# Second expert matrix loaded in 4 KB runs a partition apart, first products on neighbouring columns

## What is computed

```python
gate = jnp.sum(jax.nn.one_hot(eidx, N_EXPERTS, dtype=jnp.float32) * w[..., None], axis=1)
hg = jnp.einsum('td,edf->tef', h, p['w1'])
hu = jnp.einsum('td,edf->tef', h, p['w3'])
act = jax.nn.silu(hg) * hu * gate[:, :, None].astype(h.dtype)
routed = jnp.einsum('tef,efd->td', act, p['w2'])
```

## Time and profile before

| | |
|---|---|
| Median of three executions | 1235.48 us |
| The profiled execution, its own time | 1235.82 us |
| Its span, first to last instruction | 1234.1 us |
| Mean granted clock of TensorE | 0.983 of full |
| TensorE busy | 95% of the span |
| Bytes read from and written to memory | 322.21 MB, 33.30 MB |

### The profile page before, as it was taken

One profiled execution on the slowest core, in us unless ns is written; L12 is line 12 of the kernel. 1 busy time (PEld: TensorE's weight loads), 2 busy tenths in 40 slices (PEclk: granted clock), 3 DMA queues, 4 the chain that ended last, 5 costly groups with the idle time before them and its releaser, 6 DMA issues.

```text
span 1234.1 us, 26531 instructions
## 1 busy us (share of the span) xinstructions
PE 1167.9 (95%) x9397; PEld 847.9 (69%) x9398; DVE 563.0 (46%) x956; ACT 325.8 (26%) x633; POOL 514.3 (42%) x522
## 2 busy tenths in 40 slices
PE   4899999999999899999899999997989999899997
PEld 3599999999999899897755555544545554455542
DVE  4285676658568868337643322221112222222234
ACT  3522322323323451435121121111111111111122
POOL 2144444445448343600355444542344455344420
PEclk9899999999999899999999999998999999999999
DMA  9954345435421233548399999999999999999887
GB/s 307 324 177 147 86 146 166 140 91 160 151 81 41 69 85 101 143 168 338 127 405 410 401 397 412 411 414 415 413 411 413 411 413 399 411 415 410 342 319 267
DMA packets 149035, 337.48 MB, mean 273 GB/s; under 512 B 14807, under 2 KB 99363, under 8 KB 123369
## 3 DMA queue, kind: packets, MB, share of 16 engines
q1 hardware_dynamic: 129304, 296.57, 64.0%
q0 software_dynamic: 16656, 34.14, 7.3%
q10 hardware_dynamic: 3025, 6.07, 1.4%
HBM read 322.21 MB, written 33.30 MB: 288 GB/s over the span
## 4 chain that ended last, share of the span: by engine, by line
PE 74%; DMA 13%; issue 5%; DVE 4%; POOL 2%; SPq 1%; ACT 0%; DVEq 0%; POOLq 0%; ACTq 0%
PE ps L1882 23%; DMA w<-in_w_dram 10%; PE ps L1896 10%; PE ps L1602 9%; PE ps L1603 9%; PE ps L1604 9%; DMA ring<-in_w_ada_dram 2%; PE ps L1890 2%; PE ps L1746 1%; PE ps L1955 1%; PE ps L1615 1%; PE ps L1747 1%; PE ps L1750 1%; PE ps L1988 1%; PE ps L1544 1%
## 5 line engine op out<-in xcount | busy, mean ns | idle before, releaser
L1882 PE MATMUL ps<-w,xe 128*64 (+1 forms) x3136 | 378.2, 393 | 21.1 <-DMA w<-in_w_dram 19.2
L1882 PEld LDWEIGHTS ps<-w,xe 128*64 128x64 f32 x3136 | 221.6, 136 | 171.7 <-issue 55.8
L569 POOL TENSOR_TENSOR wsplit<-ring,wsplit 128x1024 fp32r<-128x1024 f32 x72 | 175.3, 2435 | 252.2 <-ACT wsplit L721 222.1
L1602 PE MATMUL ps<-h_s_hi,wsplit 128*128 128x260 f32 x960 | 272.3, 284 | 0.0
L1604 PE MATMUL ps<-h_s_hi,wsplit 128*128 128x260 f32 x960 | 270.8, 282 | 0.0
L1603 PE MATMUL ps<-h_lo_m_hi,wsplit 128*128 128x260 f32 x832 | 234.9, 282 | 0.0
L1464 DVE TENSOR_TENSOR rs<-sg,ps 128x128 f32<-128x128 f32 x98 | 28.2, 288 | 365.5 <-ACT sg L1051 365.5
L1602 PEld LDWEIGHTS ps<-h_s_hi,wsplit 128*128 128x128 f32 x960 | 180.8, 188 | 6.7 <-issue 5.9
L1896 PE MATMUL ps<-w,eactT 128*64 128x512 f32 (+1 forms) x784 | 184.8, 592 | 0.0
L1604 PEld LDWEIGHTS ps<-h_s_hi,wsplit 128*128 128x128 f32 x960 | 180.9, 188 | 0.0
L1603 PEld LDWEIGHTS ps<-h_lo_m_hi,wsplit 128*128 128x128 f32 x832 | 156.7, 188 | 0.0
(11 more groups left out here) (357 smaller groups left out, 1373.0 us busy)
## 6 DMA issues: line engine op xcount, KB each, us to landing
w<-in_w_dram SPq DMA_DIRECT2D x192, 1024.0 KB, 21.6
ring<-in_w_in_dram SPq DMA_DIRECT2D x56, 512.0 KB, 3.8
ring<-in_w_ada_dram SPq DMA_DIRECT2D x8, 2048.0 KB, 8.8
ring<-in_w_ada_dram SPq DMA_DIRECT2D x8, 1024.0 KB, 26.5
ring<-y_rows SPq DMA_DIRECT2D x4, 2048.0 KB, 18.2
ring<-in_w_out_a_dram SPq DMA_DIRECT2D x8, 512.0 KB, 3.6
ring<-in_w_out_b_dram SPq DMA_DIRECT2D x8, 512.0 KB, 3.5
ring<-in_w_o_dram SPq DMA_DIRECT2D x8, 512.0 KB, 3.7
```

Source lines behind the costliest of these rows:

```text
L569: pool.tensor_tensor(wsplit[:, b, 1], raw[raw_slot], wsplit[:, b, 0], ALU.subtract).then_inc(S["w_lo"], 1)
L1602: mm(ps[:, bank + h, 0:HT], wsplit[:, b, 0, k, :], hi[:, k, p:q], start=(k == 0), stop=False)
L1882: ins = mm(ps[a * STRIP:(a + 1) * STRIP, 2 + f, 0:2 * P], xe[:, k, a * STRIP:(a + 1) * STRIP], w[a][:, f, k], start=(k == 0), stop=(k == C ...
```

## The change

The load of `w2` gives partition `p` the rows p and 128 + p of the matrix, two runs of 4 KB that are 512 KB apart in memory, in place of one run of 8 KB. Its size and its place in the slot stay. With that order slice `k` of `w2` holds the hidden units 128k + p, so the up product of half `f` takes the columns from 128f on, which are neighbours in the slot. The loads of `w1` and `w3`, the number of instructions on every engine, the order of issue and the waits stay the same.

```diff
             def down_weights(e, slot):
                 sp.dma_start(w2raw[slot],
-                             w2[0, ds(e, 1), :, :].rearrange("a (p k) n -> p (a k) n", p=P)).then_inc(w2_in[slot], 16)
+                             w2[0, ds(e, 1), :, :].rearrange("a (k p) n -> p (a k) n", p=P)).then_inc(w2_in[slot], 16)
...
                         ins = mm(ps[a * STRIP:(a + 1) * STRIP, 2 + f, 0:2 * P], xe[:, k, a * STRIP:(a + 1) * STRIP],
-                                 w[a][:, f, k], start=(k == 0), stop=(k == C - 1))
+                                 w[a][:, k, :, f * P:(f + 1) * P], start=(k == 0), stop=(k == C - 1))
...
-                        up = [w6[:, ds(at_slot, 4096)].rearrange("p (m k n f) -> p f k m n", m=2, k=C, f=FT),
-                              w13[slot].rearrange("p m (k n f) -> p f k m n", k=C, f=FT)]
+                        up = [w6[:, ds(at_slot, 4096)].rearrange("p (m k n) -> p k m n", m=2, k=C),
+                              w13[slot].rearrange("p m (k n) -> p k m n", k=C)]
```

## The result

The changed kernel takes 1238.82 us (median of nine executions, 1237.71 to 1239.77), the kernel before 1235.17 us beside it: ratio 1.0021, 95% interval 1.0012 to 1.0029. It is slower, as forecast, by about 2.6 us (1.5 to 3.6), half of the forecast 5.2. The profiled execution took 1238.59 us, with a span of 1236.9 us.

What follows compares the result with a forecast made beforehand. DMA engines set the last landing TensorE waits for; four steps and the closing stage follow. Landing +4.1, steps -1.3 and clock +2.4 give +5.2 us: 1241.0 us profiled, 1240.7 us median; range 1234.0 to 1253.0 us.

Steps and rivals of the forecast that it cites:

- What bounds the kernel: Expert stage: the end is the landing TensorE waits for at 1154.6 us, plus four steps and the closing stage.
- Rival D: DMA engines have slack where it counts, so shorter steps count in full: at most -16.0 us, 1219.5 us; chance 0.12.
- Part 1: Load of w2: 128 more packets for each of 57 loads, at 8.9 ns, delay the last landing by 4.1 us.
- No gain can be there: Load of w2: no gain possible, since nothing about the bytes gets less.
- C: Load of w2: packets cost nothing extra, +0.8 us, 1236.3 us, or 1234.2 with the clock held; chance 0.18.
- E: Load of w2: the pattern costs what y_rows loads cost, +24.5 us, 1260.0 us; chance 0.10 (anywhere from 1245 to 1260).
- Part 2: Up products: neighbouring columns shorten each step by 0.33 us; only four steps behind the last landing count, -1.3 us.
- Rival B: Up products: the column stride is free, so +4.1 to +5.7 us, 1239.6 to 1241.2 us; chance 0.12.
- Part 3: Last wait for weights: it grows from 2.55 to about 5.5 us, and TensorE's clock falls behind it, +2.4 us.
- case A: Last restart: the clock holds there, +4.1 - 1.3 = +2.8 us, 1238.3 us; chance 0.10.
- The closing stage shifts as a block: End of the kernel: the closing stage has the same work and shifts as a block, as do start-up, gathers and scatters.

Runs made afterwards that it cites:

- columns alone: The kernel before with up products on neighbouring columns, w2 still loaded in one 8 KB run per partition: ratio 0.999 (0.9981 to 0.9999) to the kernel before.
- the filled wait: The changed kernel with 14 small idle matmuls ahead of the last wait for weights: ratio to the kernel before 1.0024, in a second comparison 1.0014.

## Why the prediction was right in direction and wrong in size

The direction and the mechanism in the main held: later landings, shorter steps, a loss of clock. Two terms of the sum were too large: the landing (+4.1 us, measured +2.9) and the clock (+2.4 us, measured +1.6 in the mean).

- **What bounds the kernel: right.** The end is the landing at the last restart, four steps and a closing stage. Taking some 16 us out of TensorE's steps brought the landing forward by 0.8 us; 7296 more packets ahead of it moved it back by 3.2 to 3.7. Rival D, the other side, is out. But the reading that a share of 1.00 "leaves no idle engines to speak of" was too strong: it stands at 0.94 from 701 to 716 us and at 0.76 in the last 15 us, where the landing is decided. The share "far below 1" ahead of 612 us was a rough reading too: it is 0.28 from 595 to 612 us, but 0.95 and 0.97 in two stretches of 10 us ahead of that. The engines have caught up before the steady loads begin, so the term is not changed.
- **Part 1, +4.1 us: the landing moved by 2.9.** The delay for a packet came out near the forecast 8.9 ns: 8.7 from 15104 packets at once, and 7.1 to 8.1 from the 7296 of the change itself, so this part of the term should have been 3.2 to 3.7 us. That agreement is in part luck: 8.9 was reckoned as engine time, and by the queue's rows the packets took 12 to 15 ns each of that, unless their records overlap. The other 0.4 to 0.8 us were lost in the sentence "No gain can be there": it looked only at bytes, not at the moments when an engine has nothing to do until a slot is free. Rivals C and E are out: the packets do cost, and nowhere near 50.7 ns. In w2's load the 512 KB lie between the two runs of one partition, and neighbouring partitions are 4 KB apart. Runs of 4 KB without that distance were not tried, so how the 7 to 9 ns divide between the packets and the 512 KB between them is not shown.
- **Part 2, -1.3 us on the path: right.** The last restart to the closing stage, less the loss of clock, is 1202.82 - 1155.88 - 2.88 = 44.1 us against 45.4 in before, so -1.4 unrounded. Groups of 56 at 6.04 us, least duration 378 ns, 10.84 us between steps. The waits for weights, forecast near 38 us in total, were 30.9 to 36.0 in the five profiles; groups that ran at the lower clock took part of what the shorter steps gave. The rule of the Trainium skill ("Advanced Engine Details and Errata", SBUF Cachelines), by which a step of two floats reads at full rate, does not hold for this moving operand: the same slot was read in 385 ns at the least with the step and 378 without (379 in columns alone, which changes nothing else). Rival B is out.
- **Part 3, +2.4 us: the mean is 1.6, from 0 to 2.9.** This is the step that failed as reasoning. The last wait was put at 5.5 us, "if no landing between stops TensorE first"; one did, in each of the five profiles, at 1119 to 1121 us, and the last wait was 1.3 to 4.1 us. And the line through three restarts gave the clock a dependence on the wait's length that the next profiles do not show: it held behind 3.15 and 3.58 us and fell behind 2.15, 2.20 and 2.46. What decides it stays open.
- **The sum.** +2.9 - 1.4 + 1.6 = +3.1 us, which is what span less first load says (624.6 against 621.4, +3.2), and lies in the interval of the timed ratio (+1.5 to +3.6 us). Of the 2.0 us that the forecast of 5.2 lies above this, 1.2 are in the landing and 0.8 in the clock. The number given for case A, 1238.3 us, is nearer to the result than the likeliest case, by the wrong route: it leaves the clock out and the landing too late.
- **"The closing stage shifts as a block"** was right at its price of before, since the steps did not end early enough. It is not so in the three profiles of the changed kernel, with and without the filled wait, whose steps end 1.6 us or more ahead of the first profile's: there TensorE waits for the loads of y_rows, and half to one microsecond is given back (34.6 to 35.1 us against 34.1).

What else stays open: whether the clock's loss behind the last wait is 1.6 us in the mean of unprofiled executions too. Filling that wait should have shown it, but the closing stage gives part of the gain back, and the rest is below what the timed comparisons resolve.

## What to carry to other kernels

Where DMA engines and TensorE are both full, find the last wait for a landing: ahead of it mostly the DMA work counts (0.8 us of some 16 taken from TensorE got through), behind it only the engine's. Read the DMA share in short windows ahead of that landing, since a mean of 1.00 hid 0.76 there. Two stretches of one trace with different packet sizes gave a price for a packet, 8.9 ns, that came within about a fifth of the delay measured at two numbers of packets. For terms of 1 or 2 us, take more than one profile of both kernels: the start of the stage and, in the changed kernel, the clock behind the last wait scatter by as much as the effect, while a difference between two events within the stage repeats within 0.6 us.

## What the runs showed of the hardware

A weight load in two runs of 4 KB, 512 KB apart, delays the last landing by 7 to 9 ns per 8 KB and DMA engine over one run of 8 KB (541.95 us to 545.2 and 544.8, and to 553.1 with three times the number of such packets). A moving operand of 256 floats with a step of two takes 7 ns longer than one without by the least duration (385 against 378 ns), 9 by the median (388 against 379), and 11 ns a pair (6.34 against 6.04 us for 28 pairs). TensorE's clock behind a wait for weights: after 3.58 us in the changed kernel the group of 56 ran at full clock, after 2.15 us in its fifth profile at 7.95 us, in the same kernel:

```profile
846.29 6.26 PE L1882 MATMUL ps<-w,xe 128*64 x56 [3.58 <-DMA w<-in_w_dram]
```

```profile
1121.05 7.95 PE L1882 MATMUL ps<-w,xe 128*64 x56 [2.15 <-DMA w<-in_w_dram]
```
